# Down projections of a feed-forward block: products of 128 rows as two products of 64 rows

## The reference

```python
def swiglu(x, w_gate, w_up, w_down):
    return (jax.nn.silu(x @ w_gate) * (x @ w_up)) @ w_down
h = layer_norm(DEEPNORM_ALPHA * h + 0.5 * swiglu(h, ffn1_w_gate[l], ffn1_w_up[l], ffn1_w_down[l]), ...)
```

## Time and profile before

| | us |
|---|---|
| median of 3 runs | 1984.83 |
| lowest, highest | 1984.29, 1987.94 |
| profiled execution | 1985.81 |
| its span | 1984.1 |
| PE busy | 1950.0 (98%) |
| PEld busy | 1660.8 (84%) |
| DVE busy | 1092.2 (55%) |
| ACT busy | 846.5 (43%) |
| POOL busy | 68.8 (3%) |

### The profile page before, as it was taken

One profiled execution on the slowest core, in us unless ns is written; L12 is line 12 of the kernel. 1 busy time (PEld: TensorE's weight loads), 2 busy tenths in 40 slices (PEclk: granted clock), 3 DMA queues, 4 the chain that ended last, 5 costly groups with the idle time before them and its releaser, 6 DMA issues.

```text
span 1984.1 us, 28819 instructions
## 1 busy us (share of the span) xinstructions
PE 1950.0 (98%) x10707; PEld 1660.8 (84%) x10707; DVE 1092.2 (55%) x1239; ACT 846.5 (43%) x947; POOL 68.8 (3%) x95
## 2 busy tenths in 40 slices
PE   9999999999999999999999999999999999999996
PEld 7888888888888888999999977888888888888885
DVE  4555554555445456677755756655455555544455
ACT  4444443444333334555645533444344444433342
POOL 0000000000000000300220100000000000000000
PEclk9999999999999999999999999999999999999998
DMA  8666666665565565655532056566666666555663
GB/s 276 191 190 188 188 185 190 179 189 176 190 208 195 189 231 132 210 176 150 144 98 86 22 160 253 177 189 185 190 180 188 198 188 188 190 174 187 204 197 128
DMA packets 186096, 355.21 MB, mean 179 GB/s; under 512 B 11200, under 2 KB 24096, under 8 KB 185264
## 3 DMA queue, kind: packets, MB, share of 16 engines
q1 hardware_dynamic: 184224, 345.29, 56.4%
q0 software_dynamic: 1696, 8.99, 1.4%
q10 hardware_dynamic: 112, 0.05, 0.0%
HBM read 352.18 MB, written 2.10 MB: 179 GB/s over the span
## 4 chain that ended last, share of the span: by engine, by line
PE 93%; DVE 4%; issue 1%; ACT 1%; DMA 0%; POOL 0%; SPq 0%; DVEq 0%; ACTq 0%; POOLq 0%
PE acc L366 27%; PE acc L368 26%; PE acc L367 26%; PE acc L389 3%; PE acc L391 3%; PE acc L393 3%; PE tp L718 1%; DVE resid L620 1%; PE acc L1910 1%; PE tp L1923 0%; DVE resid L828 0%; PE acc L1936 0%; PE tp L477 0%; DVE wlo L354 0%; ACT whi L347 0%
## 5 line engine op out<-in xcount | busy, mean ns | idle before, releaser
L354 DVE TENSOR_TENSOR wlo<-raw,whi 128x1024 fp32r<-128x1024 f32 (+2 forms) x652 | 780.3, 1204 | 815.5 <-ACT whi L347 815.4
L347 ACT ACTIVATE whi<-raw 128x1024 fp32r<-128x1024 f32 (+2 forms) x652 | 671.9, 1039 | 976.1 <-PE acc L368 914.5
L366 PE MATMUL acc<-whi,xT 128*128 128x512 f32 (+2 forms) x1688 | 649.0, 384 | 3.9 <-DVE wlo L354 2.3
L368 PE MATMUL acc<-whi,xT 128*128 128x512 f32 (+2 forms) x1688 | 642.8, 381 | 0.0
L367 PE MATMUL acc<-wlo,xT 128*128 128x512 f32 (+2 forms) x1688 | 642.0, 380 | 0.0
L366 PEld LDWEIGHTS acc<-whi,xT 128*128 128x128 f32 x1688 | 317.0, 188 | 70.3 <-DVE wlo L354 4.4
L368 PEld LDWEIGHTS acc<-whi,xT 128*128 128x128 f32 x1688 | 316.9, 188 | 61.1
L367 PEld LDWEIGHTS acc<-wlo,xT 128*128 128x128 f32 x1688 | 317.2, 188 | 56.9
L366 PE MATMUL acc<-whi,hT 128*128 128x512 f32 x680 | 265.7, 391 | 2.1 <-DVE resid L828 2.1
L368 PE MATMUL acc<-whi,hT 128*128 128x512 f32 x680 | 264.8, 389 | 0.0
L367 PE MATMUL acc<-wlo,hT 128*128 128x512 f32 x680 | 264.7, 389 | 0.0
(11 more groups left out here) (312 smaller groups left out, 1166.3 us busy)
## 6 DMA issues: line engine op xcount, KB each, us to landing
raw<-in_ffn_w_up_dram SPq DMA_DIRECT2D x176, 512.0 KB, 3.7
raw<-in_ffn_w_down_dram SPq DMA_DIRECT2D x176, 512.0 KB, 4.7
raw<-in_ffn_w_gate_dram SPq DMA_DIRECT2D x175, 512.0 KB, 3.8
raw<-in_w_in_dram SPq DMA_DIRECT2D x48, 512.0 KB, 3.8
raw<-in_w_out_dram SPq DMA_DIRECT2D x32, 512.0 KB, 6.6
raw<-in_w_in_dram SPq DMA_DIRECT2D x32, 260.0 KB, 2.8
raw<-in_w_in_dram SPq DMA_DIRECT2D x16, 456.0 KB, 4.6
raw<-in_w_q_idx_dram SPq DMA_DIRECT2D x8, 512.0 KB, 4.8
```

The lines of the kernel that those rows point to most:

```text
L347: act.activation(hi[:, s, :, 0:w], raw[:, r, :, 0:w], ACT.Copy).then_inc(hi_done, 1)
L354: dve.tensor_tensor(lo[:, s, :, 0:w], raw[:, r, :, 0:w], hi[:, s, :, 0:w].bitcast(F32), ALU.subtract).then_inc(lo_done, 1)
L366: pe.matmul(o, hi, w_hi[:, s, k, 0:width], start=first and k == 0, stop=False)
L368: ins = pe.matmul(o, lo, w_hi[:, s, k, 0:width], start=False, stop=last and k == UNIT_KT - 1)
```

## The change

In the two down projections each product of 128 rows becomes two of 64 rows. The upper 64 partitions of both operands give one product, into `acc0`; the lower 64 give another, into `acc1`, which the down projections had not used. The two follow each other in the program. DVE then adds both banks to the residual, one after the other; the second addition waits for the first. Before the first unit of a down projection PE also waits for `acc1` to be free of the last up chunk. The transposes, the other projections, the loads and the splits are as before.

```diff
@@ token_mm
             width = st.phases[p].width
+            if p in DN:
+                return rows_mm(pe, acc, half, stat, kt0, w_hi[:, s], w_lo[:, s], first, last)
             o = acc[:, half, 0:width]
@@ new function
+        def rows_mm(pe, acc, half, stat, kt0, w_hi, w_lo, first, last):
+
+            for k in range(UNIT_KT):
+                cols = slice(half * P, half * P + P)
+                for j, (x, w) in enumerate(((0, w_hi), (0, w_lo), (1, w_hi))):
+                    for rows, bank in ((slice(0, P // 2), acc), (slice(P // 2, P), acc1)):
+                        ins = pe.matmul(bank[:, half], stat[rows, kt0 + k, x, cols], w[rows, k],
+                                        start=first and k == 0 and j == 0, stop=last and k == UNIT_KT - 1 and j == 2)
+            return ins
@@ unit_mm
                     wait(pe, free[half], n_chunk)
+                if first and p in DN and isinstance(it, int) and it == 0:
+                    pe.wait_ge(acc1_free[half], GATE_CHUNKS * (1 + DN.index(p)))
                 if moving == "w":
@@ resid_tile
+            if p in DN:
+                dve.scalar_tensor_tensor(out=resid[:, t, cols], in0=acc1[:, t], scalar=scale,
+                                         in1=resid[:, t, cols], op0=ALU.mult, op1=ALU.add)\
+                   .then_inc(sem("lower_rows"), 1)
+                dve.wait_ge(sem("lower_rows"), T * c + (T * OUT_CHUNKS * DN.index(p) + t + 1))
             dve.scalar_tensor_tensor(out=resid[:, t, cols], in0=acc0[:, t], scalar=scale,
                                      in1=resid[:, t, cols], op0=ALU.mult, op1=ALU.add)\
                .then_inc(acc0_free[t], 1)
```

## The result

| | before | after |
|---|---|---|
| median, us | 1985.61 (4 runs) | 2000.07 (4 runs) |
| lowest, highest | 1984.29, 1987.94 | 1998.68, 2002.25 |
| profiled execution | 1985.81 | 2002.25 |
| its span | 1984.1 | 2000.5 |

The change makes the kernel slower: ratio 1.0076, 95% interval 1.0064 to 1.0089, 14.5 us between the medians. Whether the other three executions had either is not on record.

The account below looks back on a forecast made before the run. PE's own pace, 227.1 ns between down product starts, was taken as the bound. Terms 0 + 10.0 + 3.3 + 1.8 = +15.1 us took the median from 1984.83 to about 2000; 8-in-10 range 1979 to 2240.

Parts of the forecast that it names:

- The two DVE terms: DVE's second additions in the down projections: 10.0 us at six chunk changes, 3.3 us at the two projection ends.
- Step 1, the pairs: PE's 2112 down products as pairs: the row groups overlap, a pair keeps 227 ns, a change of nothing.
- The load bound of 222 to 240 ns: PE's weight loads: a pair's two loads in series need at most 222 ns, or fit in 240 ns.
- PEld's share in the down stretches: Sign of being right: the weight loads' busy share in the down stretches rises towards the whole.
- rival A: Down pairs: one row group streams while the other changes weights, hiding the 13 ns gap; 1974 us, chance 0.12.
- My estimate of 213 ns for a pair's loads: Down pairs: two loads at 107 ns each, 213 ns, leaving PE's 227 ns path 14 ns to spare.
- Step 2, the additions: DVE at chunk ends: second addition costs 0.83 us, 1.66 us per chunk change; 10.0 us, plus 3.3 at projection ends.
- The signs that I named: Each chunk change has two PE gaps, about 1.3 and 0.8 us, both released by DVE's second addition.
- Step 3, the starts: Start of each down projection: PE waits 0.9 us for acc1, twice, 1.8 us.
- Step 4, "nothing else": Rest of the kernel: DMA, splits and POOL the same, form switches around the transposes free; 0 us.
- B: Down pairs: a row group's load cannot run beside its own matmul; 338 ns a pair, about 2234 us, chance 0.15.
- C: Down pairs: no overlap of row groups in equal columns; 454 ns a pair, 2480 us, chance 0.14.

Follow-up runs that it names:

- run 1: The changed kernel with both products of a pair on the upper 64 rows, the lower rows left out: 2465.48 us.
- Run 6: The changed kernel without DVE's second addition, the lower rows' sums left out of the result: 1987.42 us, ratio 1.0012.
- run 7: The kernel before with DVE's second addition alone, all products whole, no wait for acc1: 1996.17 us, ratio 1.0059.
- runs of three: The changed kernel with three products of one row group, then three of the other, in turn within a half: 1999.15 us.
- runs of six: The changed kernel with six products of one row group, then six of the other, within a half: 2019.87 us.
- of twelve: The changed kernel with six products per row group, the second half beginning with the lower rows, so twelve stand together: 2191.50 us, ratio 1.1043.

## Why the prediction was right, point by point

The time, 2000.07 for 2000, is closer than the working deserves. The two DVE terms were 2.0 us too high, and three others 1.5 too low (0.3 at the starts, 0.6 at the switches, 0.6 with the pairs); the rest of the luck is that the four runs of before have a median 0.8 us above the one that I added to.

*Step 1, the pairs.* Right, both in mechanism and in size: 227.3 ns for 227. The choice of "nothing" between -26 and +27 was carried by the mixer's quadrants, and run 1 shows its ground, the row groups. The load bound of 222 to 240 ns was no bound, and my sentence that PEld's share in the down stretches would rise was wrong: it was 196.21 of 240 us before and 194.80 of 239 now, 82% both times. Loads of the two groups run beside each other too. The timeline, two pairs of loads of 184 ns each in 0.41 us, with a pair of matmuls beside them:

```profile
600.32 0.39 PE L379 MATMUL acc<-wlo,hT 64*128 64x512 f32 x2
600.32 0.41 PEld L379 LDWEIGHTS acc<-whi,hT 64*128 64x128 f32 x4
```

So rival A's stop, "two loads in series need 222", was not what kept the gap; the gap belongs to each lane, as run 1 has it (227 ns in one group alone). My estimate of 213 ns for a pair's loads, worked out from the rule of the Trainium skill ("TensorE: Matmul & The Clock Gate", section on LDWEIGHTS) as if they were in series, does not apply. The rule's part on rows agrees with the trace: a load of 64 rows lasts 184 ns where one of 128 lasts 188. Its time, 107 ns for 128 columns, is not what these records last.

*Step 2, the additions.* Right in kind, 13.3 for 11.3: six changes at 1.42 instead of 1.66 and two ends at about 1.4. The term was mis-sized because I took the price of an addition from a bn_stats that waits for one (0.83); an addition that waits for an addition starts after 0.71. Run 6 takes the step out and run 7 puts it in alone: 12.7 (12.0 against its own before) and 11.8 us. The signs that I named, gaps of about 1.3 and 0.8 us, came out at 1.2 (1.41 less 0.23) and 0.5 to 0.7.

*Step 3, the starts.* 2.1 for 1.8. I had the first product 0.70 us after the start of DVE's multiplications (half of 1.28, and 0.06); it started 0.83 after (502.48, 503.31).

*Step 4, "nothing else".* Not right: the switches around the transposes cost 0.6, and the clock of 1.2 GHz after the first block 1.4 in the profiled execution. I had read the mixer's change of form as free, from a line that does not resolve 0.15 us.

*The rivals.* All three are out by the 227.3 ns, where A (gap hidden) had 215, B 338 and C (no overlap) 454. B is out by the loads too: they begin while matmuls of both groups run, 3 to 4 ns after these begin, as in the earlier trace rows. The rule of the Trainium skill that B rested on ("only when row_grp differs") did not hold in the cut array either: both row groups were in use at 600.32, and loads ran. A pair of 220 ns, at which A's gain would have begun, was 7 ns away.

## What to carry to other kernels

Cutting a full product in two row groups buys no time where both halves still stream all columns; it doubles the accumulators, and the engine that empties them has twice the additions. If those banks are free, let the chunks alternate between them: that took the emptying off the path here and gained 2.1 us. Price an added instruction by the pair of operations it will really stand between, and look at the granted clock behind each idle time that it lengthens.

## What the runs showed of the hardware that I had not expected

Matmuls of different row groups start out of the program's order: with runs of three the interleaving costs nothing (1999.15 against 2000.07), with runs of six 20 us, of twelve 191 us. The Trainium skill, "TensorE: Matmul & The Clock Gate", Part 3, has matmuls in strict order of start; the record at 570.378 in the runs of six stands against it. Two products of 64 rows and 512 columns start 3 to 4 ns apart, which agrees with that Part's 4 ns. Their loads overlap as well, and the two switches from 64 to 128 rows and back cost 0.32 us around the transposes (1.34 against 1.02).
